# Output products laid out by rows of tokens, with norms along the free axis and h turned back by transposes

## The chip, the cores and the metric

One core of a Trainium2 chip (trn2) runs one program. The metric is the device time of that program in microseconds (us), the median of a few runs; lower is better. TensorE (PE) does the matrix products, VectorE (DVE), ScalarE (ACT) and GpSimd (POOL) the rest, and SyncE (SP) issues the weight transfers. All data are fp32.

## The reference, cut to what matters

Sequence 512, model width 1024, batch 1. Two layers of one block (three mixing branches, then a gated feed-forward net), then two layers of another (three branches only). What the change touches is what stands at the end of each of the six sub-layers, and at the start of the next:

```
for l in range(2):                          # first block
    h = rmsnorm(x, norm_mix_pre[l])
    ... three branches from h @ w_in[l] ...
    merged = g0 * y_ret + g1 * y_sc + g2 * y_cf
    x = x + rmsnorm(merged @ w_o[l], norm_mix_post[l])
    h = rmsnorm(x, norm_ffn_pre[l])
    up = causal_dwconv(h @ w_up[l], ffn_conv_w[l])        # 2 * 2816 wide
    gate, val = split(up)
    x = x + rmsnorm((silu(gate) * val) @ w_down[l], norm_ffn_post[l])
for l in range(2):                          # second block
    h = rmsnorm_2(x, pre_norm_g[l])
    ... three branches from h @ w_in[l], merged ...
    x = x + rmsnorm_2(merged @ w_out[l], post_norm_g[l])

rmsnorm(x, g) = x * rsqrt(mean(x * x over the 1024 channels) + 1e-6) * g
```

## The kernel before, in words

**Products.** Every fp32 product is made of three passes of a faster 32-bit format (F32R): each operand is split into a high and a low part, and `three` issues high x high, high x low and low x high into one PSUM bank. A weight chunk (128 x 1024 fp32, 512 KB) goes one road: SP loads it into one of 4 `raw` buffers when the low part of the chunk 4 before is cut; ACT casts the high part into one of 4 places (L903); DVE subtracts to get the low part (L1319). A place comes free when the last matmul on the chunk that was in it is done ("closed"). ACT and DVE work in program order, and cut chunks `LA` = 2 ahead of the product that they stand beside.

**Layout.** x, h and all tiles lie with the channels across the partitions: 8 tiles of 128 channels x 512 tokens. A product tile is 128 output channels x 512 tokens; weights are stationary, tokens move.

**Boundaries.** Between two sub-layers stands a boundary, numbered B = 0 to 6 in the code: 0 is the start (x to h), 1 and 3 follow the mixers of the first block, 2 and 4 its feed-forward nets, 5 and 6 the layers of the second block. At each of 1 to 6 the output product (`wo`, or `dn` for the feed-forward net) gives y; its squares are summed over the channels, which here lie across partitions. So ACT squares each tile (L1007), DVE adds them up (L1453), TensorE sums over the partitions with products by ones (`columns`, 128x1), DVE and POOL make the root on a column (L1334, L1829: a power of -0.5), and TensorE spreads it again over the partitions (`rows`, 128x128, against the identity). Then DVE renews x (L1423, L1426). The same chain with x in place of y gives h: squares on ACT (L967), sums on POOL (L1903), then h times the gain on DVE (L1437), its high part on ACT (L975), its low part on DVE and POOL (L1329, L1908).

**Order by hand.** The chain is run twice, for tokens 0 to 255 (hf = 0) and 256 to 511 (hf = 1). The first 2 output tiles (5 after a feed-forward net, `NFULL`) are made whole, the rest in halves of 256 tokens: first all left halves, then all right ones, beside which the steps of the first half's chain stand, one at each point (`beside_tail`). The weights of these tiles are kept (`KEPT`) or, after a feed-forward net, loaded twice (chunks `dn..b`). Some low parts of chunks are cut by POOL there (L1841, `POOL_LOW`). When the output product is over, three products of the next sub-layer are made early (`EARLY`): their first half (`early_first`) covers the chain of the second half, then `early_second` does the other half, k by k over all three.

After boundaries 1 and 3 follow the products `upg0`, `upv0`, `upg1`, ... of the feed-forward net. ACT's order there is: scaled copies of `upg0` and `upv0` (L1115), a sigmoid (L1120), the high part of the product of both (L980, which waits for the taps on DVE, L1583, and for POOL's L1971), and only then the casts of the next chunks. After boundaries 4 and 5 follow `cq0` to `cq2`, `ckv0`, `ckv1`: ACT copies the tiles, squares those of `cq`, POOL adds the squares (L1879), and TensorE's `columns` for them stands ahead of its product `ckv1`.

## Time and profile before

| | us |
|---|---|
| median of 3 runs | 3441.5 (3439.97 to 3445.51) |
| the profiled execution | 3445.09 |
| its span in the profile | 3443.7 |
| TensorE busy (matmuls) | 3328.8 (97%) |
| VectorE busy | 1801.6 (52%) |
| ScalarE busy | 1228.6 (36%) |
| GpSimd busy | 465.0 (14%) |

The span runs from the first to the last instruction of one execution. TensorE is busy in nearly all of it, so the time is its work plus the places where it waits. Its matmuls overlap in the records: the pace is read from the starts of neighbours, not from the length of one. PEclk is the clock that TensorE was granted, as a share of full speed (0.5 is 1.2 GHz, 1.0 is 2.4 GHz).

### The profile page before, as it was taken

How to read it: one execution, taken by the hardware profiler on the slowest of the kernel's cores; microseconds unless marked ns; L12 is line 12 of the kernel's file. 1: busy time of each engine (PE TensorE's matmuls, PEld its weight loads, DVE VectorE, ACT ScalarE, POOL GpSimd, SP SyncE). 2: the span in 40 equal slices, each digit the busy share in tenths (PEclk: the TensorE clock that was granted, in tenths of full speed). 3: DMA queues.
4: the chain of work that ended last, by engine and by line, in shares of the span. 5: the costliest groups of instructions: out<-in, count | busy, mean ns of one | idle time of the engine just before them, and what ended most of it. 6: DMA issues, size and time to landing. Idle time of an engine off the chain costs nothing.

```text
span 3443.7 us, 38725 instructions
## 1 busy us (share of the span) xinstructions
PE 3328.8 (97%) x15780; PEld 2743.6 (80%) x15780; DVE 1801.6 (52%) x2514; ACT 1228.6 (36%) x1886; POOL 465.0 (14%) x398
## 2 busy tenths in 40 slices
PE   7999989999899998999989999999998999999998
PEld 6788888888778888888877678888887658888887
DVE  3784556653577555665354442446545444344744
ACT  3232344333323234433343232226534332223742
POOL 2101121100310112111041000110013000011000
PEclk9999999999999999999999999999999999999999
DMA  4223212233322322223321132323231113222222
GB/s 147 68 80 104 92 68 92 98 104 118 112 70 78 104 95 70 92 98 100 118 93 54 53 104 86 103 81 101 89 108 60 54 62 104 88 96 87 96 93 76
DMA packets 90049, 309.81 MB, mean 90 GB/s; under 512 B 10160, under 2 KB 10416, under 8 KB 89872
## 3 DMA queue, kind: packets, MB, share of 16 engines
q1 hardware_dynamic: 87552, 299.50, 26.4%
q0 software_dynamic: 2320, 7.82, 0.7%
q8 instruction: 127, 2.08, 0.3%
q14 instruction: 50, 0.41, 0.0%
HBM read 305.18 MB, written 2.10 MB: 89 GB/s over the span
## 4 chain that ended last, share of the span: by engine, by line
PE 90%; DVE 4%; ACT 3%; POOL 2%; issue 1%; DMA 0%; SPq 0%; POOLq 0%; DVEq 0%; ACTq 0%
PE ps L454 90%; POOL f L1903 1%; ACT wh L903 1%; DVE wl L1319 1%; DVE X L1426 1%; DVE f L1423 0%; ACT r L975 0%; DVE r L1329 0%; PE ps L798 0%; DVE f L1437 0%; POOL sm L1829 0%; ACT f L1176 0%; DMA raw<-wst 0%; ACT r L980 0%; POOL wl L1841 0%
## 5 line engine op out<-in xcount | busy, mean ns | idle before, releaser
L454 PE MATMUL ps<-r,wh 128*128 128x512 f32 (+1 forms) x8584 | 2530.1, 379 | 35.6 <-DVE r L1329 22.5
L454 PEld LDWEIGHTS ps<-r,wh 128*128 128x128 f32 x8584 | 1588.1, 191 | 333.2 <-issue 34.0
L454 PE MATMUL ps<-r,wl 128*128 128x512 f32 (+1 forms) x4292 | 1617.3, 377 | 0.0
L454 PEld LDWEIGHTS ps<-r,wl 128*128 128x128 f32 x4292 | 820.4, 191 | 145.1
L1319 DVE TENSOR_TENSOR wl<-raw,wh 128x1024 fp32r<-128x1024 f32 (+3 forms) x565 | 700.4, 1255 | 326.3 <-ACT wh L903 324.9
L903 ACT CAST wh<-raw 128x1024 fp32r<-128x1024 f32 (+3 forms) x574 | 564.2, 999 | 598.6 <-PE ps L454 597.4
L980 ACT CAST r<-f 128x512 fp32r<-128x512 f32 x182 | 112.0, 620 | 508.1 <-DVE f L1590 146.8
L1500 DVE TENSOR_TENSOR f<-f,ps 128x512 f32<-128x512 f32 x96 | 66.0, 688 | 388.7 <-PE ps L454 386.3
L1941 POOL TENSOR_TENSOR f<-f,f 128x512 f32<-128x512 f32 x64 | 114.5, 1791 | 752.4 <-DVE f L1500 752.4
L1329 DVE TENSOR_TENSOR r<-f,r 128x512 fp32r<-128x512 f32 (+1 forms) x230 | 150.2, 658 | 120.9 <-ACT r L980 115.8
L454 PE MATMUL ps<-f,f 128*128 128x128 f32 (+7 forms) x640 | 201.6, 450 | 7.6 <-DVE f L1661 4.3
L454 PEld LDWEIGHTS ps<-f,f 128*128 128x128 f32 (+1 forms) x640 | 105.9, 198 | 105.9 <-issue 79.9
L1343 DVE SCALAR_TENSOR_TENSOR f<-f,vt,f 128x511 f32<-128x511 f32 (+29 forms) x240 | 174.7, 791 | 0.0
L1583 DVE SCALAR_TENSOR_TENSOR f<-ps,vt,f 128x511 f32<-128x511 f32 (+1 forms) x176 | 131.4, 748 | 73.6 <-ACT f L1115 70.5
L454 PE MATMUL ps<-wh,r 128*128 128x512 f32 x448 | 143.2, 397 | 0.0
L987 ACT COPY f<-ps 128x512 f32<-128x512 f32 x100 | 58.3, 588 | 196.7 <-PE ps L454 196.7
L1453 DVE TENSOR_TENSOR f<-f,f 128x256 f32<-128x256 f32 (+1 forms) x72 | 37.2, 516 | 162.6 <-ACT f L1007 162.3
L454 PE MATMUL ps<-r,r 128*128 128x256 f32 x960 | 118.4, 284 | 0.0
L454 PEld LDWEIGHTS ps<-r,r 128*128 128x128 f32 x960 | 116.5, 192 | 0.3
L1971 POOL TENSOR_TENSOR f<-f,f 128x512 f32<-128x512 f32 x44 | 56.6, 1287 | 411.7 <-DVE f L1583 411.7
L999 ACT ACTIVATE f<-ps,vt 128x256 f32<-128x256 f32 (+1 forms) x78 | 40.8, 523 | 192.3 <-PE ps L454 192.0
L1115 ACT ACTIVATE f<-ps,vt 128x512 f32<-128x512 f32 x88 | 60.2, 687 | 135.1 <-PE ps L454 135.1
(132 smaller groups left out, 1786.2 us busy)
## 6 DMA issues: line engine op xcount, KB each, us to landing
raw<-wst SPq DMA_DIRECT2D x500, 512.0 KB, 3.3
raw<-wst SPq DMA_DIRECT2D x48, 320.0 KB, 3.0
raw<-wst SPq DMA_DIRECT2D x38, 384.0 KB, 3.1
f<-tab POOLq DMA_DIRECT2D x16, 256.0 KB, 4.5
X<-x_in SPq DMA_DIRECT2D x4, 512.0 KB, 6.4
f<-gmb POOLq DMA_DIRECT2D x4, 512.0 KB, 4.4
raw<-wst SPq DMA_DIRECT2D x8, 256.0 KB, 3.0
out<-X SPq DMA_DIRECT2D x8, 256.0 KB, 2.0
```

The source lines that it names most:

```text
L454: return e.matmul(o, a, b, start=start, stop=stop, skip_group_check=True)
L903: e.copy(h[:, 0:WIDTH[c]], raw[:, c % NRAW, 0:WIDTH[c]]).then_inc(*hi_cut.up(("hi", c)))
L980: e.copy(r, f).then_inc(*act_hi.up(event))
L987: e.copy(dst, bank(key)).then_inc(*act_tile.up(event, ("free", key)))
L1115: e.activation(F(60 + 3 * (j % 3) + m), bank(key), ACT.Copy, scale=vec1(L, "fcw", 3 * (22 * m + j) + 2)[:, 0:1]).then_inc(*act_tile.up(("f ...
L1319: e.tensor_tensor(l[:, 0:WIDTH[c]], raw[:, c % NRAW, 0:WIDTH[c]], h[:, 0:WIDTH[c]].bitcast(F32), ALU.subtract).then_inc(*lo_cut.up(("lo", c)))
L1329: e.tensor_tensor(lo, f, hi.bitcast(F32), ALU.subtract).then_inc(*dve_lo.up(event))
L1343: e.scalar_tensor_tensor(out=C, in0=F(16 + j)[:, 0:S - s], scalar=vec1(L, "cfw", 31 * j + i)[:, 0:1], in1=C, op0=ALU.mult, op1=ALU.add).th ...
L1500: e.tensor_tensor(F(M + j) if begins else q, q, bank(key), ALU.mult).then_inc(*dve_tile.up(("free", key), *events))
L1583: e.scalar_tensor_tensor(out=q[:, s:S], in0=bank(key)[:, 0:S - s], scalar=vec1(L, "fcw", 3 * (22 * m + j) + 2 - s)[:, 0:1], in1=q[:, s:S], ...
L1941: e.tensor_tensor(F(M + j), F(M + j), F(ring[j % 3]), ALU.add).then_inc(*pool_sum.up(*events))
L1971: e.tensor_tensor(F(t + 1), F(t), F(t + 1), ALU.mult).then_inc(*pool_tile.up(("f_prod", L, j)))
```

## The change

The output products are turned round. The tokens (128 of them) are the stationary operand and 512 columns of the weights move, so y comes out as rows of tokens: 4 tiles t of 128 tokens, each in two banks n of 512 channels. x is stored so from the start (`x_in` and `out` are laid out so too). The norms are then sums along the free axis: ACT squares and sums in one instruction (`accum_out`), DVE adds the two halves and epsilon (`mean`), POOL takes the root of one column (`roots`), and DVE applies it as a scalar of each partition, with gains that are loaded as rows (`gains`, 1 MB a boundary, 0.5 MB at boundary 0). `columns` and `rows` are gone from the boundaries, and so is POOL's share of sums and low parts. h comes out as rows too, and is turned back by transposes on TensorE, 8 a tile and 32 a boundary (`turn_rows`); ACT and DVE cut its parts straight from PSUM.

The products go over tiles 0 and 1 first, then over 2 and 3. For `wo` the 8 chunks stay in place for both passes (5 in kept places, 3 in the ring). The feed-forward net's `dn` has 22 chunks of 1024 columns, one for each k, and all are read twice (44 instead of 33 chunks; of the 33, 11 had 768 columns). Four products of the next sub-layer are made early instead of three, and `early_second` goes over the products by halves of k, so that they end one after the other.

```diff
-NFULL = {1: 2, 2: 5, 3: 2, 4: 5, 5: 2, 6: 2}
-DN_PARTS = (range(0, 8), range(8, 16), range(16, 22))
+NF = 22
+WO = [(c, n) for c in range(4) for n in range(2)]
...
+    def output(L, w, l):
+        for c, n in WO:
+            out.append((f"{L}/wo{c}{n}", [(w, l, (2 * c + i) * P, P, rng(512 * n, 512)) for i in range(2)]))
...
+        for hf in range(2):
+            for k in range(NF):
+                out.append((f"{l}/dn{hf}_{k}", [("w_down", l, k * P, P, (0, 1024))]))
...
-EARLY = {0: ["0/ca0", "0/cb0", "0/ca1"], 1: ["0/upg0", "0/upv0", "0/upg1"], 2: ["1/ca0", "1/cb0", "1/ca1"],
...
-POOL_LOW = _pool_low()
+EARLY = {0: ("0/ca0", "0/cb0", "0/ca1", "0/cb1"), 1: ("0/upg0", "0/upv0", "0/upg1", "0/upv1"),
...
+         4: ("2/cq0", "2/cq1", "2/cq2", "2/ckv0"), 5: ("3/cq0", "3/cq1", "3/cq2", "3/ckv0")}
+ROWS_AT = {"y": 0, "new0": 1, "new1": 3, "x0": 5, "x1": 7, "turn0": 7, "turn1": 8, "lo0": 9, "lo1": 10}
...
             def early_second(B):
-                for k in range(8):
-                    xh, xl = h_half(B, 1, k)
+                for a in range(2):
                     for name in EARLY[B]:
                         h, l = split_at(NAME[name])
-                        last = three(bank(name)[:, halves(1)], h[:, k * P:(k + 1) * P], l[:, k * P:(k + 1) * P], xh, xl,
-                                     k == 0, k == 7)
-                        if k == 7:
+                        for k in range(4 * a, 4 * a + 4):
+                            xh, xl = h_half(B, 1, k)
+                            last = three(bank(name)[:, halves(1)], h[:, k * P:(k + 1) * P], l[:, k * P:(k + 1) * P], xh, xl,
+                                         k == 0, k == 7)
+                        if a:
                             banks.let_go(name)
                             last.then_inc(*group_done.up(("done", name), ("closed", NAME[name])))
+            def turn_rows(B, t):
+                H = ROWS_T[B][2]
+                for a in range(2):
+                    key = ("tr", B, t, a)
+                    o = take_from(key, ("y", B, t, a)) if B else take(key)
+                    w.wait_ge(*at("landed", "cst"))
+                    w.wait_ge(*at("h_out", B, t, a))
+                    for i in range(4):
+                        last = e.transpose(o[:, i * P:(i + 1) * P], F(H[a])[:, i * P:(i + 1) * P], ident)
+                    last.then_inc(*group_done.up(("done", key)))
+            def rows_by(B, t, n, ks, xs, h, l, cols, last_k, closes=None):
+                ts = slice(t * P, (t + 1) * P)
+                for k, c in zip(ks, cols):
+                    last = three(bank(("y", B, t, n)), xs[k][0][:, ts], xs[k][1][:, ts], h[:, c:c + S], l[:, c:c + S],
+                                 k == 0, k == last_k)
...
+                if B in FFN:
+                    for k in range(NF):
+                        dn(B, xs, (0, 1), k)
+                    rows((2, 3))
+                    for k in range(NF - 4):
+                        dn(B, xs, (2, 3), k)
+                        for t in range(2):
+                            if k == ROWS_AT[f"turn{t}"]:
+                                turn_rows(B, t)
+                    for t in (2, 3):
+                        for k in range(NF - 4, NF):
+                            dn(B, xs, (t,), k)
+                else:
+                    for c, n in WO:
+                        wo(B, xs, (0, 1), c, n)
+                    rows((2, 3))
+                    for c, n in WO:
+                        wo(B, xs, (2,), c, n)
+                    if B < 6:
+                        turn_rows(B, 0)
+                    for n in range(2):
+                        for c in range(4):
+                            wo(B, xs, (3,), c, n)
+                        if n == 0 and B < 6:
+                            turn_rows(B, 1)
+                if B < 6:
+                    after(B, ("e0", "e1", "e2", "t2", "t3", "e3") if B in FFN else ("e0", "t2", "e1", "e2", "t3", "e3"))
...
+            def squares(B, t, kind):
+                for n in range(2):
...
+                    e.activation(F(ROWS_T[B][3]), bank(key) if kind == "y" else xt(t, n), ACT.Square, scale=1.0 / 32,
+                                 accum_out=stat(t)[:, m:m + 1]).then_inc(*act_square.up(("squares", kind, B, t, n)))
+            def h_hi(B, t):
+                for a in range(2):
+                    w.wait_ge(*at("done", ("tr", B, t, a)))
+                    e.copy(parts(0, t, a), turned(("tr", B, t, a))).then_inc(*act_hi.up(("h_hi", B, t, a)))
...
+            def mean(B, t, kind):
+                m = 0 if kind == "y" else 4
+                w.wait_ge(*at("squares", kind, B, t, 1))
+                e.tensor_scalar(stat(t)[:, m + 2:m + 3], stat(t)[:, m:m + 1], stat(t)[:, m + 1:m + 2], EPS, ALU.add,
+                                ALU.add).then_inc(*dve_col.up(("mean", kind, B, t)))
+            def renew(B, t):
+                w.wait_ge(*at("root", "y", B, t))
+                w.wait_ge(*at("landed", f"gain{B}"))
+                for n in range(2):
...
+                    e.scalar_tensor_tensor(out=F(T[n]), in0=bank(key), scalar=stat(t)[:, 3:4], in1=gain(B, 0, n), op0=ALU.mult,
+                                           op1=ALU.mult).then_inc(*dve_tile.up(("y_out", B, t, n), ("free", key)))
+                    e.tensor_tensor(xt(t, n), xt(t, n), F(T[n]), ALU.add).then_inc(*dve_tile.up(("x_new", B, t, n)))
+            def h_out(B, t):
+                H = ROWS_T[B][2]
+                w.wait_ge(*at("root", "x", B, t))
...
+                for n in range(2):
+                    if t:
+                        w.wait_ge(*at("done", ("tr", B, t - 1, n)))
+                    e.scalar_tensor_tensor(out=F(H[n]), in0=xt(t, n), scalar=stat(t)[:, 7:8], in1=gain(B, 1, n), op0=ALU.mult,
+                                           op1=ALU.mult).then_inc(*dve_tile.up(("h_out", B, t, n)))
+            def h_lo(B, t):
+                for a in range(2):
...
+                    e.tensor_tensor(parts(1, t, a), turned(key), parts(0, t, a).bitcast(F32), ALU.subtract).then_inc(
+                        *dve_lo.up(("h_lo", B, t, a), ("free", key)))
...
+            def boundary(B):
...
+                    mean(B, 2, "y")
+                    cut(e0 + 1)
+                    renew(B, 2)
+                    cut(e0 + 3)
+                    mean(B, 3, "y")
+                    mean(B, 2, "x")
+                    renew(B, 3)
+                    h_out(B, 2)
+                    mean(B, 3, "x")
+                    h_out(B, 3)
+                    h_lo(B, 2)
+                    h_lo(B, 3)
+                    return
...
+            def roots(B, *which):
+                for kind, t in which:
+                    root(stat(t)[:, m:m + 1], stat(t)[:, m + 1:m + 2], 1, at("mean", kind, B, t), ("root", kind, B, t))
+            def gains(B):
+                e.dma_start(F(ROWS_T[B][0], 4), gains_in[B]).then_inc(*landed(f"gain{B}"))
```

On TensorE, at the end of the first feed-forward net's output product, where its last right half is followed by the second half's chain (the one product of ones, the one spread) and by `early_second`, stood:

```order
L454 MATMUL ps<-r_512_66,wh 128x256
L454 MATMUL ps<-r_512_65,wl 128x256
L454 MATMUL ps<-ct,f_512_85 128x1 x2
L454 MATMUL ps<-ct,sm 128x128 x2
L454 MATMUL ps<-r_512_51,wh 128x256
L454 MATMUL ps<-r_512_52,wh 128x256
L454 MATMUL ps<-r_512_51,wl 128x256
```

In the same place of the changed kernel the third early product is followed by the transposes of tiles 2 and 3 (L550, from the tiles of h by rows) and by the first half of the fourth:

```order
L445 MATMUL ps<-h_8192_52,wh 128x256 x2
L445 MATMUL ps<-h_8192_52,wl 128x256
L550 MATMUL ps<-ct,f_512_56 128x128 x4
L550 MATMUL ps<-ct,f_512_127 128x128 x4
L550 MATMUL ps<-ct,f_512_56 128x128 x4
L550 MATMUL ps<-ct,f_512_127 128x128 x4
L445 MATMUL ps<-h_8192_52,wh 128x256 x2
L445 MATMUL ps<-h_8192_52,wl 128x256
```

The two places where TensorE met the chain have become two sets of transposes, next to each other, ahead of the last 24 matmuls that can cover anything.

On ScalarE, in the same stretch, the last steps of both chain halves stood so (L903 casts a chunk, L999 and L1007 take a last half of y, L962 and L967 square x, L975 cuts h):

```order
L975 CAST r_512_65<-f_512_67 128x256
L999 ACTIVATE f_512_186<-ps,vt 128x256
L1007 ACTIVATE f_512_84<-ps 128x256
L903 CAST wh<-raw 128x1024
L962 ACTIVATE f_512_85<-X 128x256
L967 ACTIVATE f_512_50<-X 128x256
L967 ACTIVATE f_512_67<-X 128x256
```

and now stand so, from the last casts of `dn` on (L893 casts a chunk, L956 squares, from `ps` for y and from `X` for x, L962 cuts h):

```order
L893 CAST wh<-raw 128x1024 x9
L956 ACTIVATE f_512_71,sm<-ps 128x512 x2
L893 CAST wh<-raw 128x1024 x2
L956 ACTIVATE f_512_71,sm<-X 128x512 x2
L893 CAST wh<-raw 128x1024 x2
L956 ACTIVATE f_512_71,sm<-ps 128x512 x2
L956 ACTIVATE f_512_71,sm<-X 128x512 x2
L962 CAST h_8192_52<-ps 128x4x128 x4
```

The squares of y of tile 3 (the third L956 row) stand behind the squares of x of tile 2 and behind two casts.

## Rows read from the trace of the kernel before

**Rows 1.** Page, part 4: the chain that ended last, by engine
```profile
PE 90%; DVE 4%; ACT 3%; POOL 2%; issue 1%; DMA 0%; SPq 0%; POOLq 0%; DVEq 0%; ACTq 0%
```

**Rows 2.** Windows of boundaries 1, 2, 5, 6 and 0
```profile
core 0: us, PE busy (x) PEld busy (x) DVE busy (x) ACT busy (x) POOL busy (x), PEclk, DMA share, GB/s
440.77:522.64 81.87, 70.83 (x513) 67.53 (x512) 43.56 (x86) 35.31 (x73) 21.04 (x27) 0.96 0.19 65
748.68:910.43 161.75, 150.69 (x904) 136.21 (x902) 71.81 (x105) 56.41 (x93) 33.77 (x38) 0.96 0.35 116
...
2536.22:2620.52 84.30, 71.92 (x514) 68.38 (x512) 46.60 (x104) 36.29 (x76) 22.09 (x29) 0.94 0.23 75
3382.67:3435.15 52.48, 48.62 (x353) 45.73 (x351) 21.43 (x40) 17.69 (x35) 3.09 (x3) 0.99 0.09 30
13.18:42.58 29.40, 21.70 (x124) 20.04 (x125) 16.13 (x30) 13.58 (x29) 16.09 (x22) 0.88 0.28 92
```

**Rows 3.** Timeline of TensorE in boundary 1: start, us, engine, operation
```profile
445.54 0.40 PE L454 MATMUL ps<-r,wl 128*128 128x512 f32 x1
...
453.06 0.39 PE L454 MATMUL ps<-r,wl 128*128 128x512 f32 x1
453.28 14.55 PE L454 MATMUL ps<-r,r 128*128 128x256 f32 x120
```

**Rows 4.** Groups by line and shape, whole run: count, busy us, mean ns
```profile
L454 PE MATMUL ps<-ct,f 128*128 128x1 f32 x208 | 28.9, 256 | 35.8 <-POOL f L1903 23.1 <-DVE f L1453 9.8 <-POOL f L1879 2.9
L798 PE MATMUL ps<-ct,f 128*128 128x128 f32 x160 | 21.3, 275 | 3.2 <-DVE f L1686 3.1
L1176 ACT ACTIVATION_READ_ACCUMULATOR f<-ps,sm 128x1 f32 x64 | 13.0, 203 | 0.0
L1007 ACT ACTIVATE f<-ps 128x512 f32<-128x512 f32 x12 | 7.1, 590 | 0.0
L980 ACT CAST r<-f 128x512 fp32r<-128x512 f32 x182 | 112.0, 620 | 508.1 <-DVE f L1590 146.8 <-POOL f L2003 139.8 <-DVE f L1752 51.3
L903 ACT CAST wh<-raw 128x1024 fp32r<-128x1024 f32 x480 | 496.8, 1046 | 518.0 <-PE ps L454 516.9 <-DMA raw<-wst 1.0
L1319 DVE TENSOR_TENSOR wl<-raw,wh 128x1024 fp32r<-128x1024 f32 x474 | 613.3, 1307 | 273.3 <-ACT wh L903 272.5
L1637 DVE SCALAR_TENSOR_TENSOR f<-f,ps 128x512 f32<-128x512 f32 x16 | 11.0, 688 | 49.2 <-ACT f L1143 49.2
L1829 POOL TENSOR_TENSOR sm<-sm 128x2 f32<-128x2 f32 x24 | 18.2, 759 | 250.6 <-DVE sm L1334 250.6
L1887 POOL TENSOR_TENSOR sm<-sm 128x1 f32<-128x1 f32 x8 | 12.2, 1529 | 141.7 <-DVE sm L1401 141.7
```

**Rows 5.** Timeline of boundary 2, at the first half's root
```profile
869.78 0.89 POOL L1829 TENSOR_TENSOR sm<-sm 128x2 f32<-128x2 f32 x1
870.82 1.20 PE L454 MATMUL ps<-ct,sm 128*128 128x128 f32 x4 [2.85 <-POOL sm L1829]
871.66 0.77 PE L454 MATMUL ps<-r,wh 128*128 128x256 f32 x2
```

**Rows 6.** Timeline of the first feed-forward net's start
```profile
528.60 1.04 ACT L903 CAST wh<-raw 128x1024 fp32r<-128x1024 f32 x1
...
531.00 0.70 PE L454 MATMUL ps<-r,wh 128*128 128x512 f32 x2 [2.73 <-issue]
```

**Rows 7.** Timeline of the second block's first layer, its start
```profile
1778.19 2.87 POOL L1879 TENSOR_TENSOR f<-f,f 128x512 f32<-128x512 f32 x2 [9.02 <-ACT f L945]
...
1781.20 1.03 PE L454 MATMUL ps<-ct,f 128*128 128x1 f32 x8 [1.46 <-POOL f L1879]
```

**Rows 8.** DMA view of the first 45 us, rate in 40 slices
```profile
GB/s 0 63 330 211 291 368 284 386 334 416 422 411 379 149 269 266 233 164 0 0 0 0 0 0 0 0 222 244 0 0 0 0 0 0 15 0 66 335 244 306
```

**Rows 9.** Window inside boundary 2, where halves take whole chunks
```profile
832.00:857.00 25.00, 25.00 (x208) 24.71 (x207) 13.01 (x17) 10.72 (x17) 3.82 (x3) 1.00 0.50 166
```

**Rows 10.** Timeline of the end: the last renewal of x
```profile
3441.19 0.42 DVE L1426 TENSOR_TENSOR X<-X,f 128x256 f32<-128x256 f32 x1
```

More of the change, by code:

```diff
@@ L1020, in boundary @@
[L1020 to L1028 removed]
+                e0 = NAME[EARLY[B][0]] if B < 6 else len(CHUNKS)
@@ L1484, in gate_proj @@
+                cut(e0 + 3)
+                mean(B, 3, "y")
+                renew(B, 3)
+                mean(B, 3, "x")
+                h_lo(B, 2)
+                h_out(B, 3)
+                h_lo(B, 3)
             def gate_proj(L, b, g, p, first=0, kind="one", cut_merged=None):
```

608 lines of the change are left out of this document (238 added, 370 removed).

## The prediction

> **What bounds the kernel now.** I read the chain of waits first: TensorE is 90% of it [rows 1], so a change pays where TensorE works less or waits less, and nowhere else. The change is all at the boundaries, so the next view is the busy time in a window around each [rows 2], from the first matmul of the output product to the last of the early products. Then the pace. Between two records of the same kind lie 33 matmuls of 512 columns: (453.06 - 445.54) / 33 = 0.228 us each; 120 matmuls of 256 columns take 14.55 us, 0.121 each [rows 3]. Two halves cost 0.014 us more than a whole. At 0.228, `wo` needs 192 matmuls of 512 columns and three early products 72: 264 x 0.228 = 60.2 us. `dn` needs 528, with the early ones 600 x 0.228 = 136.7. What a window is longer than that is the price of the boundary:
>
> - 1: 81.9 - 60.2 = 21.7. 3 repeats it within 0.1 us.
> - 2: 161.8 - 136.7 = 25.1. 4 repeats it within 0.2 us.
> - 5: 84.3 - 60.2 = 24.1.
> - 6: 52.5 - 43.8 = 8.7, no early products.
>
> That is 126 us. Idle TensorE is the larger part (81.9 - 70.8 = 11.0 us in boundary 1, 11.1 in 2, 12.4 in 5, 3.9 in 6) [rows 2]. The rest is small products (28.9 us for 208 of one column, 0.14 each [rows 4]; a boundary has 16 records of them and 16 of the spreads, some 4 us), halves (2 to 3 us), and a slow clock.
>
> **The clock.** The granted clock is 0.94 to 0.96 in those windows [rows 2]; at 0.96, 8% of 82 us ran at the lower level of 1.2 GHz, which loses 3 us. It shows behind the waits: TensorE stood 2.85 us for the root until 870.82, and right behind it two matmuls of 256 columns take 0.77 us [rows 5], where the pace above is 0.24. In boundary 6, whose idle time is 3.9 us in all, the clock stayed at 0.99 [rows 2].
>
> **The change part by part.**
>
> *Removed.* All of the price above, in all boundaries: products by ones, spreads, the waits around them, the halves of the output products, the low parts on POOL.
>
> *Transposes.* 32 at each of boundaries 0 to 5. The 160 of the trace keep TensorE busy for 21.3 us, 0.133 each [rows 4]: 4.3 us a boundary. The Trainium skill ("TensorE: Matmul & The Clock Gate", Part 4: PE-mode transpose) gives some 275 ns for a transpose in a kernel's context. The trace has the mean of 275 ns for one record too, but 160 of them overlap to 21.3 us, so the record's length is not the pace; by the page's figure the 192 would cost 27 us more than in my sum.
>
> *Early products.* Four in halves: 192 matmuls of 256 columns, 192 x 0.007 = 1.3 us over whole ones. The fourth product itself is work taken from behind the boundary.
>
> *Waits in the wo boundaries (1, 3, 5).* Time 0 is the end of the pass over tiles 0 and 1; tile 2 takes 48 matmuls, 10.9 us. Squares with a sum: 0.59 + 0.20 each half [rows 4], 1.8 us a tile with the wait between; both tiles done at 3.8. `mean` on DVE is a column operation, 0.15; POOL's root 0.76 (another form with one column has 1.53, both in [rows 4]; I take 0.76, the same line's, and keep 0.8 us x 4 roots on the chain as the upper end). `renew` is four DVE operations of 0.69: tile 0 at 7.0, tile 1 at 9.8. `mean` and root of x: 11.0. `h_out` 11.7 and 12.5. TensorE wants to turn tile 0 at 10.9: it waits about 1.5 us. Tile 1 is ready when wanted. The end of the product is at about 25; on DVE the chain of tile 3 then runs squares 27.0, root 29.0, renewal 31.8, squares of x 32.8, root 34.1, low parts of tile 2 34.5, `h_out` 35.9. Covered are 4 x 2.9 us of early products less the last: TensorE is at 34.7 and waits 1 us. The first output tile, which before needed all eight merged tiles at once, now needs the last two only in its seventh chunk. With a margin of 1.5 us for hand-overs I take 4 us idle, and the clock of boundary 6, since the idle time is that of boundary 6. Price: 4.3 + 1.3 + 4 = 9.6.
>
> *Waits in the FFN boundaries (2, 4).* ACT does the squares of y of tile 3 only behind the squares of x of tile 2, and behind two casts. With time 0 at the end of the product: cast of the first early chunk at -3.5 (its place closes at -4.1), second cast done at -1.4, their low parts on DVE (1.3 us) done at +0.1, renewal of tile 2 at 2.9, its squares at 3.9, two casts of 1.05 [rows 4] at 6.0, squares of y of tile 3 at 7.8, root 9.1, renewal 12.1, `h_out` of tile 2 13.5, of tile 3 16.2. TensorE has three halves of 2.9 us: it is done at 9.3 (0.6 waited for a chunk), waits 3.7 for tile 2 and 1.4 more for tile 3, and only then comes the fourth half. Idle 6.2, with hand-overs 7, and behind a wait of 3.7 the clock falls as it does in [rows 5]: 2.5 us. Price: 4.3 + 1.3 + 7 + 2.5 = 15.1.
>
> *The chunks.* 44 in place of 33 a net. A chunk now carries 12 matmuls, 2.7 us. ACT's cast is 1.05 and DVE's 1.31 of that [rows 4]. In the window from 832 to 857 halves already took a chunk of 1024 columns in 24 x 0.121 = 2.9 us, TensorE was busy in all of it at 166 GB/s [rows 9], and the transfers of the start ran at over 400 GB/s [rows 8]. 512 KB in 2.7 us is 192 GB/s. In the second pass DVE's steps stand between the cuts; the tightest low part is done 0.8 us ahead of its use. I cost it at nothing; if that cover is gone, each 0.1 us a chunk costs 88 x 0.1 = 9 us.
>
> *Behind the boundary.* What follows is now late. The fourth early product used to cover (5.5 us) what ACT has to do before the next cast. Boundaries 1 and 3: before, the cast began at 528.60 and TensorE waited until 531.00, 2.7 us [rows 6]; that is 8.4 us from the end of the early products at 522.64 [rows 2]. Now `upv0` ends 2.9 us before the boundary's end and its taps are on DVE 1 us sooner: ready 4.7 us after it. 2 us more, and 1.5 for the clock: 3.5 each. Boundary 2: 0.3. Boundaries 4 and 5: POOL's sums of squares end at 1781.06 and TensorE had waited 1.46 us with `ckv0` before it [rows 7]. From the last copy of `cq` to there are 6 us; `cq2` now ends 1.5 us before the boundary's end, so TensorE stands 5.2 us with nothing: 3.7 more, 1.3 for the clock: 5 each.
>
> *Boundary 0.* Before, 42.6 - 13.2 us [rows 2], with three products. Now rows are normed as they land, but ACT's and DVE's orders put the first casts between the tiles; tile 3's transposes are at about 29 and the four products end at about 48, which is 42.6 plus the fourth product. Nothing.
>
> *Boundary 6.* TensorE ends 8.7 us sooner less 0.4 for a chunk: 8.3. From its last matmul the span had 8.5 us, of them a renewal in 16 small steps to 3441.6 [rows 10]. Now squares 1.8, mean, root 1.1, renewal 2.8, transfer 2.5: the same.
>
> **The sum.** 1 and 3: 21.7 - 9.6 - 3.5 = 8.6 each, 17.2. 2: 25.1 - 15.1 - 0.3 = 9.7. 4: 25.2 - 15.1 - 5 = 5.1. 5: 24.1 - 9.6 - 5 = 9.5. 6: 8.3. 0: 0. Together 49.8. The profiled execution took 3445.1 us, so 3395; it lay 3.6 us above the median of the runs, so against the median 3391.5. I say 3391.
>
> Bounds: the transposes at 0.12 (a matmul of 256 columns) to 0.14 (one of one column) -2 to +1; the squares' sum at nothing more than the copy's 0.59, -2 a boundary, the casts out of PSUM with a stride at 0.59 to 1.05, up to +2 a boundary, +10; roots at 1.53 +3 a boundary, +18; idle at nothing, -25 with its clock; the second pass short of chunks by a cover of 0.1 us, +9. Not all fall together: the forecast's own range is 3372 to 3410.
>
> **The rivals.**
>
> *The chain is not shorter, only elsewhere (half the gain).* For it: each tile crosses ACT, DVE, POOL, DVE, ACT, DVE, POOL, DVE, TensorE, ACT, DVE, and each queue holds it behind other steps; four tiles instead of two halves. Against it: tiles 0 and 1 are hidden by whole passes, and only tile 3's chain is bare. With 5 us more idle and 2 us more slow clock in five boundaries: 35 us given back, 3426.
>
> *Slower: the ring of chunks.* The feed-forward products wait for weights, one chunk after another, since a raw buffer comes free only when DVE has cut the chunk 4 before. It decides from the chunk's own time: 49.8 / 88 = 0.57, so a supply slower than 2.7 + 0.57 = 3.3 us a chunk, or 159 GB/s, eats all, and at 3.6 us a chunk the kernel takes 88 x 0.9 - 50 = 29 us more, 3471. For it: no stretch before has ever wanted 192 GB/s for 120 us. Against it: [rows 9] held 166 GB/s with TensorE full.
>
> *More than that: the waits vanish.* If the hand-overs are as short as the best of the trace, only transposes and halves stay: 3391 - 25 = 3366.
>
> *It does not do what it says.* If the order of rows did not let tile 0 and 1 go ahead (their renewal stuck in DVE's queue behind cuts that wait for places), the boundary has the chain of all four tiles bare: about 20 us idle each, no gain, 3440.
>
> **How the numbers follow.** Forecast 0.60 (3391); half the gain 0.22 (3426); waits vanish 0.09 (3366); ring 0.05 (3471); no effect 0.04 (3440). Range 3366 to 3428: it leaves out the ring, no effect, and parts of the other two. A measurement here tells 0.2%, 7 us. Faster needs less than 3434.6: the forecast, the waits gone and nearly all of the half gain, 0.91. Same: most of the no-effect case, 0.04. Slower 0.05.
>
> **What would show it.** Windows of the same shape around the boundaries: longer than 60.2 by about 10 us for `wo`, than 136.7 by 15 for `dn` (one more early product adds 5.5 to each). TensorE waits ahead of L550: 1.5 us once in a wo boundary, near 4 and 1.4 in an FFN one, with ACT's L956 on `ps` in front of them. A wait of nearly 5 us at each start of `ffn` and 5 us ahead of the `cq` sums. No wait of a `wh,r` product for L893 or L1305 inside `dn`. The forecast is wrong in its largest term if such waits appear in `dn`, or if the waits ahead of L550 sum to over 10 us.

## The result, and the profile after

| | before | after |
|---|---|---|
| median, same chips | 3443.09 us (4 runs) | 3366.84 us (4 runs, 3362.54 to 3367.42) |
| the profiled execution, its span | 3445.09, 3443.7 | 3367.42, 3366.1 |
| mean granted clock of TensorE | 0.982 | 0.989 |

The ratio is 0.9776, with a 95% interval of 0.9759 to 0.9793: 76 us faster, where 50 were forecast. Against the 3441.5 us that the prediction was worked out from, that ratio gives 3364.4. The busy times and the chain of waits of the changed kernel (L445 is `three`, L893 the cast, L1305 the low part, L1424 `h_out`, L550 the transposes):

```profile
PE 3296.2 (98%) x14952; PEld 2681.3 (80%) x14952; DVE 1795.5 (53%) x2353; ACT 1212.4 (36%) x1800; POOL 363.3 (11%) x288
...
PE 94%; DVE 2%; ACT 2%; issue 1%; POOL 0%; DMA 0%; SPq 0%; ACTq 0%; POOLq 0%; DVEq 0%
```

TensorE's share of the chain went from 90% [rows 1] to 94%, and DVE, ACT and POOL together from 9% to 4%. TensorE's busy time fell too (3328.8 to 3296.2 us). Windows of boundaries 1, 2, 5, 6 and 0, cut as in [rows 2] from the first matmul of the output product to the last early one:

```profile
435.83:506.43 70.60, 70.53 (x417) 62.33 (x415) 39.47 (x57) 28.51 (x55) 8.89 (x11) 1.00 0.27 90
731.69:885.67 153.98, 148.72 (x753) 126.95 (x751) 82.75 (x92) 66.93 (x92) 10.01 (x17) 0.99 0.54 179
2483.23:2553.83 70.60, 70.52 (x417) 62.32 (x415) 39.61 (x71) 29.89 (x58) 9.64 (x12) 1.00 0.31 104
3314.90:3358.78 43.88, 43.80 (x193) 35.77 (x191) 17.92 (x24) 11.34 (x21) 3.88 (x5) 1.00 0.26 96
12.30:48.59 36.29, 32.23 (x224) 30.65 (x225) 16.61 (x24) 14.72 (x25) 5.11 (x10) 1.00 0.41 150
```

These hold four early products: 288 x 0.228 = 65.6 us are needed in a `wo` window, 624 x 0.228 = 142.3 in a `dn` window. The price of a boundary is now 70.6 - 65.6 = 5.0 us in 1, 3 and 5 (forecast 9.6) and 154.0 - 142.3 = 11.7 in 2, 11.5 in 4 (forecast 15.1). In a `wo` window TensorE is busy in all but 0.1 us, at the full clock.

Stage by stage, from the start of each output product to the next (the last to the end of the span):

| from, to | before | after | change | forecast |
|---|---|---|---|---|
| start, B1 | 440.8 | 435.8 | -4.9 | 0 |
| B1, B2 | 307.9 | 295.9 | -12.1 | -8.6 |
| B2, B3 | 555.6 | 541.4 | -14.2 | -9.7 |
| B3, B4 | 307.9 | 295.4 | -12.5 | -8.6 |
| B4, B5 | 924.0 | 914.7 | -9.3 | -5.1 |
| B5, B6 | 846.5 | 831.7 | -14.8 | -9.5 |
| B6, end | 61.0 | 51.2 | -9.8 | -8.3 |

Together -77.6 us of span against -49.8 forecast. Each stage gave more than forecast, by 1.5 to 5.3 us.

The transposes in boundary 1, on TensorE:

```profile
468.37 0.62 PE L445 MATMUL ps<-r,r 128*128 128x512 f32 x2
468.83 1.03 PE L550 MATMUL ps<-ct,f 128*128 128x128 f32 x8
469.62 0.48 PE L445 MATMUL ps<-wh,r 128*128 128x512 f32 x1
```

No idle time stands before them. From the first of 8 to the next product are 0.79 us, 0.099 each; one follows the other at 0.109, and `double_turn` below gives 0.11 for one more. I count 0.11. In boundary 2 (TensorE, then ACT, then POOL) two waits are left:

```profile
864.08 0.28 PE L445 MATMUL ps<-h,wl 128*128 128x256 f32 x1
866.70 1.23 PE L550 MATMUL ps<-ct,f 128*128 128x128 f32 x8 [2.34 <-DVE f L1424]
868.81 1.97 PE L550 MATMUL ps<-ct,f 128*128 128x128 f32 x8 [0.89 <-DVE f L1424]
870.43 0.78 PE L445 MATMUL ps<-h,wh 128*128 128x256 f32 x2
871.00 0.41 PE L445 MATMUL ps<-h,wl 128*128 128x256 f32 x1
```

```profile
858.18 0.63 ACT L956 ACTIVATE f<-X 128x512 f32<-128x512 f32 x1 [0.66 <-DVE X L1415]
...
858.81 1.98 ACT L893 CAST wh<-raw 128x1024 fp32r<-128x1024 f32 x2
860.70 0.58 ACT L956 ACTIVATE f<-ps 128x512 f32<-128x512 f32 x1
...
861.40 0.60 ACT L956 ACTIVATE f<-ps 128x512 f32<-128x512 f32 x1
```

```profile
867.41 0.55 POOL L1851 TENSOR_TENSOR sm<-sm 128x1 f32<-128x1 f32 x1 [3.91 <-DVE sm L1402]
```

The order on ACT is the one that the prediction named: squares of x of tile 2, two casts, then the squares of y of tile 3. The matmuls behind the wait show the clock: two of 256 columns in 0.57 us, start to start, where [rows 3] have 0.24. Behind boundary 1 stands what [rows 6] had, and there is a wait near the start of `dn` that the prediction did not have (TensorE, and ACT at the second place):

```profile
506.31 0.28 PE L445 MATMUL ps<-h,wl 128*128 128x256 f32 x1
511.17 1.19 PE L445 MATMUL ps<-h,wh 128*128 128x512 f32 x2 [4.59 <-issue]
512.16 0.63 PE L445 MATMUL ps<-h,wl 128*128 128x512 f32 x1
...
736.90 0.39 PE L445 MATMUL ps<-wh,r 128*128 128x512 f32 x1
739.33 0.47 PE L445 MATMUL ps<-wh,r 128*128 128x512 f32 x1 [2.04 <-ACT wh L893]
...
1727.58 0.56 PE L445 MATMUL ps<-ct,f 128*128 128x1 f32 x2 [5.21 <-POOL f L1883]
```

```profile
732.47 0.62 ACT L1104 ACTIVATE f<-f 128x512 f32<-128x512 f32 x1
736.40 0.62 ACT L967 CAST r<-f 128x512 fp32r<-128x512 f32 x1 [3.31 <-DVE f L1604]
736.93 3.88 ACT L893 CAST wh<-raw 128x1024 fp32r<-128x1024 f32 x4
```

ACT begins its sigmoid at 732.47 and then stands 3.31 us, for DVE's product of the taps, at the cast of that product (L967). Four chunk casts are queued behind it, in order, and the third chunk of `dn` is one of them. The waits behind boundaries 4 and 5 are those of [rows 7] grown from 1.46 to 5.21 us.

**Where 77.6 us came from.** TensorE idle, the span less its busy time: 3443.7 - 3328.8 = 114.9 us before, 3366.1 - 3296.2 = 69.9 after, -45. The mean clock of 0.982 before comes from 122 us at half speed, of which half is lost, 61; after there are 77 us of it, 39 lost: -22. The 192 records of small products are gone (0.111 each by `small_back` below): -21. The 192 transposes: +21. Some 970 pairs of halves in the output products are gone (0.0114 each by `halved_rows`): -11. The fourth early product is in halves: +2. That is -76. The first two terms are read from the traces, no run takes them away one by one, and they overlap a little, since a slow stretch can fall on idle time.

### The profile page after: what moved, and what is told of

Its sections match the earlier page's. It is cut to its first block, busy times and chain, and to the rows that moved or that the text cites. A ratio compares the mean times of both kernels' runs of the same rounds, so it can differ in the third digit from the quotient of the medians.

```text
span 3366.1 us, 36633 instructions
## 1 busy us (share of the span) xinstructions
PE 3296.2 (98%) x14952; PEld 2681.3 (80%) x14952; DVE 1795.5 (53%) x2353; ACT 1212.4 (36%) x1800; POOL 363.3 (11%) x288
## 4 chain that ended last, share of the span: by engine, by line
PE 94%; DVE 2%; ACT 2%; issue 1%; POOL 0%; DMA 0%; SPq 0%; ACTq 0%; POOLq 0%; DVEq 0%
PE ps L445 93%; DVE wl L1305 1%; ACT wh L893 1%; PE ps L550 1%; PE ps L792 0%; DMA raw<-wst 0%; DVE f L1597 0%; ACT f L1160 0%; DVE f L1412 0%; POOL f L1883 0%; DVE f L1359 0%; POOL f L1961 0%; ACT r L967 0%; DVE f L1424 0%; DVE f L1700 0%
## 5 line engine op out<-in xcount | busy, mean ns | idle before, releaser
L445 PE MATMUL ps<-h,wh 128*128 128x512 f32 (+1 forms) x5824 | 1717.1, 379 | 14.0 <-issue 13.0
L445 PEld LDWEIGHTS ps<-h,wh 128*128 128x128 f32 x5824 | 1074.5, 190 | 216.6 <-issue 20.4
L445 PE MATMUL ps<-h,wl 128*128 128x512 f32 (+1 forms) x2912 | 1098.4, 377 | 0.0
L1305 DVE TENSOR_TENSOR wl<-raw,wh 128x1024 fp32r<-128x1024 f32 (+3 forms) x596 | 745.3, 1265 | 358.3 <-ACT wh L893 356.7
L893 ACT CAST wh<-raw 128x1024 fp32r<-128x1024 f32 (+3 forms) x596 | 593.1, 1008 | 686.9 <-PE ps L445 671.8
L445 PEld LDWEIGHTS ps<-h,wl 128*128 128x128 f32 x2912 | 552.8, 190 | 100.1
L445 PE MATMUL ps<-r,wh 128*128 128x512 f32 x1632 | 507.3, 392 | 1.2 <-DVE f L1359 1.2
L445 PEld LDWEIGHTS ps<-r,wh 128*128 128x128 f32 x1632 | 305.3, 188 | 68.5 <-issue 6.4
L445 PE MATMUL ps<-r,wl 128*128 128x512 f32 x816 | 317.7, 389 | 0.0
L445 PE MATMUL ps<-wh,r 128*128 128x512 f32 x960 | 305.1, 392 | 4.4 <-ACT wh L893 4.1
L967 ACT CAST r<-f 128x512 fp32r<-128x512 f32 x182 | 112.1, 620 | 515.1 <-DVE f L1604 146.8
L445 PEld LDWEIGHTS ps<-wh,r 128*128 128x128 f32 x960 | 180.2, 188 | 44.7 <-ACT wh L893 4.9
L445 PE MATMUL ps<-f,f 128*128 128x128 f32 (+7 forms) x640 | 201.1, 449 | 7.6 <-DVE f L1675 4.3
L445 PEld LDWEIGHTS ps<-f,f 128*128 128x128 f32 (+1 forms) x640 | 105.8, 197 | 105.4 <-issue 79.5
L445 PE MATMUL ps<-wl,r 128*128 128x512 f32 x480 | 186.8, 389 | 0.0
L445 PEld LDWEIGHTS ps<-r,wl 128*128 128x128 f32 x816 | 153.2, 188 | 32.2
```

The source lines that it names most:

```text
L445: return e.matmul(o, a, b, start=start, stop=stop, skip_group_check=True)
L893: e.copy(h[:, 0:WIDTH[c]], raw[:, c % NRAW, 0:WIDTH[c]]).then_inc(*hi_cut.up(("hi", c)))
L967: e.copy(r, f).then_inc(*act_hi.up(event))
L1305: e.tensor_tensor(l[:, 0:WIDTH[c]], raw[:, c % NRAW, 0:WIDTH[c]], h[:, 0:WIDTH[c]].bitcast(F32), ALU.subtract).then_inc(*lo_cut.up(("lo", c)))
```

## The experiments

All times are medians beside runs of the kernel before on the same chip; ratios are against it. The changed kernel's is 0.9776. A slow stretch is time in which TensorE was granted half its clock.

**late_squares**: in boundaries, the squares of y of tiles 0 and 1 begin only when the whole pass is done.

```diff
                     if kind == "y":
+                        if t < 2:
+                            w.wait_ge(*at("done", ("y", B, 1, 1)))
                         w.wait_ge(*at("done", key))
```

> The changed kernel, in which ACT squares y of tiles 0 and 1 only when the last bank of tile 1 is done. In the changed kernel the first halves of both tiles are squared one chunk earlier, which I had left out. If an early start of the chain was all that kept TensorE from waiting ahead of the first transposes of the wo boundaries, the wait of 1.5 us that I forecast is back in boundaries 1, 3 and 5, with some slow clock: about 3372. If my durations for the chain were too long as well (roots of 0.55 us in place of 0.76, squares of 0.78 a half in place of 0.9), about 2 us of slack are left, the wait is under 0.5 us and the time stays at 3366 to 3368.

3365.9 us, ratio 0.9768 (0.9751 to 0.9784): nothing. Its chain of boundary 1, on ACT, DVE and TensorE:

```profile
458.15 0.60 ACT L958 ACTIVATE f<-ps 128x512 f32<-128x512 f32 x1 [7.81 <-PE ps L445]
...
467.58 1.41 DVE L1426 SCALAR_TENSOR_TENSOR f<-X,sm,f 128x512 f32<-128x512 f32 x2 [0.66 <-POOL sm L1853]
...
468.84 1.03 PE L550 MATMUL ps<-ct,f 128*128 128x128 f32 x8
```

From the end of the pass (435.8 + 96 x 0.228 = 457.7) `h_out` of tile 0 now ends at 469.0, 11.3 us later; the prediction had 12.5 for both halves, and a wait of 1.5. The steps were shorter than the prediction's, and the early start of the squares only adds reserve: the second of the two outcomes named.

**double_turn**: each transpose twice.

```diff
-                    for i in range(4):
+                    for i in list(range(4)) * 2:
```

> The changed kernel with each transpose of h issued twice (the second writes the same place): 192 more. If a transpose costs TensorE what its neighbours' starts show in the changed kernel (8 of them in 0.79 us, 0.10 each), 19 us more, a little less where they fall into a wait: 3383 to 3387. If it costs its record's length, 0.275 us, 53 us more: 3420.

3376.4 us, 0.9805 (0.9791 to 0.9820): 10 us more, under the 3383 to 3387 expected. In boundary 1:

```profile
468.31 1.91 PE L550 MATMUL ps<-ct,f 128*128 128x128 f32 x16
469.98 0.48 PE L445 MATMUL ps<-wh,r 128*128 128x512 f32 x1
```

16 transposes take 1.67 us where 8 took 0.79, 0.11 for each more. The span grew by 13.4 us, TensorE's idle time fell from 69.9 to 66.9, and the slow stretches from 77.3 to 75.3 us, worth 1.0: together some 17 us for 192 transposes, 0.09 each. At the record's length of 0.27 it would have been 52.

**small_back**: one fp32 product by one column and one of 128 columns put ahead of each four transposes.

```diff
+                    e.matmul(o[:, 0:1], F(H[a])[:, 0:P], ident[:, 0:1], start=True, stop=True)
+                    e.matmul(o[:, 0:P], F(H[a])[:, 0:P], ident, start=True, stop=True)
                     for i in range(4):
```

> The changed kernel with the small products put back: ahead of each set of four transposes one fp32 product by a single column and one of 128 columns against the identity, 8 of each a boundary (boundaries 0 to 5), 192 records in all, as many as the change took out of the boundaries. Their results are overwritten by the transposes. Theory (they cost TensorE only their own time, 0.10 to 0.13 us a record as the transposes do): 19 to 25 us more, less 1 to 2 us where they stand in a wait: 3384 to 3391 us. Rival (a small fp32 product between matmuls of the split format costs its record of 0.25 to 0.275 us, or the change of format costs more): 192 x 0.26 = 50 us more, 3417 us.

3380.53 us, 0.9815 (0.9802 to 0.9829): 13 us more, under the 19 to 25 expected. In boundary 1:

```profile
470.25 0.28 PE L549 MATMUL ps<-ct,f 128*128 128x1 f32 x2
...
470.69 0.60 PE L552 MATMUL ps<-ct,f 128*128 128x128 f32 x4
...
471.93 0.48 PE L445 MATMUL ps<-wh,r 128*128 128x512 f32 x1
```

Eight transposes with their eight small records take 1.68 us from the first to the next product, where the transposes alone took 0.79: 0.111 a record, as the theory has it. The span grew by 12.4 us, idle time fell by 5.2 (69.9 to 64.7), and the slow stretches fell from 77.3 to 74.5 us, worth 1.4: 19 us together for 192 records, 0.10 each. So the size per record holds; what the forecast had too small was the idle time that the small products would fill (1 to 2 us). The clock moves the time on its own, too: matmul by matmul the run is 17.3 us behind the changed kernel at 2713 us and 12.4 at 2770, because the changed kernel has a slow stretch of 10.2 us there that this one has not.

**halved_rows**: each output-product matmul as two of 256 columns. Its output products are not the sums of the reference; number and shape of its matmuls are as the edit says.

```diff
+                    for q in (0, 256):
-                    last = three(bank(("y", B, t, n)), xs[k][0][:, ts], xs[k][1][:, ts], h[:, c:c + S], l[:, c:c + S],
+                        last = three(bank(("y", B, t, n))[:, q:q + 256], ..., h[:, c + q:c + q + 256], l[:, c + q:c + q + 256],
...
```

> The changed kernel with every output-product matmul of 512 columns made as two of 256 columns (1824 of them become 3648). This sizes the term of halves that the change took out of the output products. Theory (pace 0.228 us for 512 columns, 0.121 for 256, so 0.014 us a pair): 1824 x 0.014 = 25.5 us more, about 3392 us, and the windows of the output products longer by 2.7 us (wo, 192 pairs) and 7.4 us (dn, 528 pairs). Rival (a half costs more than the pace of 256 columns shows, because each needs its own weight load of 128 columns, which no longer hides): 0.03 us a pair or more, over 3421 us.

3388.63 us, 0.9835 (0.9822 to 0.9849): 20 us more. Its boundary 6:

```profile
3327.65:3373.72 46.07, 46.07 (x385) 46.02 (x383) 17.92 (x24) 11.32 (x21) 3.88 (x5) 1.00 0.24 92
```

46.07 - 43.88 = 2.2 us for 192 pairs, 0.0114 a pair (0.014 forecast), and 1824 x 0.0114 = 21 us. The halves' own weight loads stay hidden (46.02 us of them within 46.07 of matmuls).

**three_early**: three early products, in the old order of `early_second`, all else as changed.

```diff
-EARLY = {0: ("0/ca0", "0/cb0", "0/ca1", "0/cb1"), 1: ("0/upg0", "0/upv0", "0/upg1", "0/upv1"),
+EARLY = {0: ("0/ca0", "0/cb0", "0/ca1"), 1: ("0/upg0", "0/upv0", "0/upg1"),
...
-                    after(B, ("e0", "e1", "e2", "t2", "t3", "e3") if B in FFN else ("e0", "t2", "e1", "e2", "t3", "e3"))
+                    after(B, ("e0", "e1", "e2", "t2", "t3") if B in FFN else ("e0", "t2", "e1", "e2", "t3"))
...
```

> The changed kernel with three early products and the old order of early_second (k by k over all three). If the row layout makes the gain, and the fourth product mostly moves waits: each of boundaries 1 to 5 waits about 2.5 us for the cuts of tile 3's h, but the starts behind the boundaries wait 2.9 and 1.6 us instead of 4.6 and 5.3 and keep the faster clock: within 10 us of the changed kernel either way, 3356 to 3376. If the fourth product is what pays, 15 to 30 us of the gain are lost: 3382 to 3397.

3353.28 us, 0.9736 (0.9722 to 0.9751): 14 us faster than the changed kernel, and 3 us under the 3356 to 3376 of the first outcome. At the end of boundary 1 and behind it:

```profile
492.94 0.47 PE L445 MATMUL ps<-h,wh 128*128 128x256 f32 x2 [0.95 <-DVE h L1431]
...
503.53 0.70 PE L445 MATMUL ps<-h,wh 128*128 128x512 f32 x2 [1.72 <-DVE f L1597]
...
510.02 0.70 PE L445 MATMUL ps<-h,wh 128*128 128x512 f32 x2 [0.78 <-issue]
```

Three short waits in place of one of 4.59, and after none of them the matmuls run at half pace (0.70 us for two here, 1.19 there). The mean clock is 0.992 against 0.989. So the fourth early product, as it was built in and with the order of `early_second` that came with it, cost 14 us. The two were not taken apart.

**before_four**: the kernel before with four early products and their `early_second`; the fourth product's chunk is cut just ahead of the step that makes h of the second half.

```diff
-EARLY = {0: ["0/ca0", "0/cb0", "0/ca1"], 1: ["0/upg0", "0/upv0", "0/upg1"], 2: ["1/ca0", "1/cb0", "1/ca1"],
+EARLY = {0: ["0/ca0", "0/cb0", "0/ca1", "0/cb1"], 1: ["0/upg0", "0/upv0", "0/upg1", "0/upv1"],
...
+                early_first(B, 3)
+                for step in steps[xrow:]:
```

> The kernel before with that part alone: four early products, early_second by halves of k, one product after the other; the fourth stands ahead of the spread of the root of x. If the fourth product is what pays: 3443 - 20 = 3423. If the row layout pays and this moves waits: a microsecond or two less in each boundary, 2 to 5 us more behind boundaries 1, 3, 4 and 5: 3438 to 3452.

3475.68 us, 1.0092 (1.0077 to 1.0107): 32 us slower, far outside what was expected. Around boundary 1 the waits up to the last products by ones are all still there, with one of 0.5 us more. The 1.13 us before the last spread is gone, but 1.43 us stands in its place, ahead of the fourth product, and the 1.56 us behind the spread is still there (TensorE, and DVE's low part of the fourth product's chunk):

```profile
514.80 0.47 PE L455 MATMUL ps<-r,wh 128*128 128x256 f32 x2 [1.43 <-issue]
521.43 0.48 PE L455 MATMUL ps<-r,wh 128*128 128x256 f32 x2 [1.56 <-DVE r L1336]
```

```profile
513.49 1.21 DVE L1326 TENSOR_TENSOR wl<-raw,wh 128x1024 fp32r<-128x1024 f32 x1
```

The profile names no releaser for the 1.43, but the low part ends at 514.70 and TensorE begins at 514.80, and in boundaries 2 to 5 it is the same to 0.1 us: most likely the fourth product came too late for its own chunk, by this edit's order. Behind boundaries 1 and 3 stand 4.58 us and behind 4 and 5 5.20, as in the changed kernel. Idle time grew by 15 us (114.9 to 129.9) and slow stretches by 19 (122 to 141), worth 9.5. These and the halves of the fourth product are 26 of the 30 us of its span; the rest was not placed. So the run shows that this fourth product does not pay in the kernel before, not that none could.

**ffn_cut**: ACT and DVE cut one more chunk ahead of the wait for the taps (both engines, one line each).

```diff
                             *act_tile.up(("f_tap", L, j, m, 0)))
+                    cut(NAME[f"{L}/upv{j}"] + LA + 1)
                     w.wait_ge(*at("f_tap", L, j, 0, 2))
...
```

> The changed kernel; in each step j of the feed-forward net ACT and DVE cut the next chunk right after the copy and the taps of upv_j, and no longer behind the product's high and low part. Theory: the wait of 4.6 us behind boundaries 1 and 3 is ACT's queue order (the cast stands behind a wait for DVE and POOL), and so is the wait of 2.2 us at the third chunk of dn. Then both go down to under 1 us, with the slow clock behind the first: 12 us of waits and 3 to 6 of clock, 3348 to 3353. Rival: the chunk's place or its transfer comes late: no change, 3366.

3347.04 us, 0.9722 (0.9708 to 0.9737): 0.0054 of 3443, or 19 us faster, a little more than expected. TensorE behind boundary 1, and ACT in front of it:

```profile
505.58 0.70 PE L445 MATMUL ps<-h,wh 128*128 128x512 f32 x2 [0.66 <-issue]
```

```profile
502.68 1.04 ACT L893 CAST wh<-raw 128x1024 fp32r<-128x1024 f32 x1
503.61 0.64 ACT L1105 ACTIVATE f<-f 128x512 f32<-128x512 f32 x1
507.45 0.62 ACT L967 CAST r<-f 128x512 fp32r<-128x512 f32 x1 [3.20 <-DVE f L1606]
```

ACT waits as long as before, but the cast stands ahead. TensorE's 4.59 became 0.66, and the 2.04 in `dn` is gone as well: one cause for both, twice each. The four waits together shrank by 11.9 us, and the slow stretches from 77 to 60 us, worth 9.

**norm_shift**: the sums for the `cq` norm taken a few products later.

```diff
-                tile(f"{L}/ckv1", xs)
-                tile(f"{L}/kr", xs)
+                tile(f"{L}/ckv1", xs, beside=False)
+                small_step("n_root", L, "q")
+                tile(f"{L}/kr", xs, beside=False)
+                small_step("n_apply", L, "q")
```

> The changed kernel; in the second block TensorE's steps of the q and k norms (products by ones, spreads) stand one product later each. Theory: the wait of 5.3 us behind boundaries 4 and 5 is for POOL's sums, while ckv1 could run; its own chunk is there 1 to 2 us after the boundary. Then the wait is 1 to 2 us, and with less slow clock 3353 to 3359. Rival: ckv1 has to wait for its chunk as long, or the wait moves to the next product: 3363 to 3367.

3354.92 us, 0.9743 (0.9729 to 0.9758): 11 us faster. Of the 5.21 us, twice, what is left there, on TensorE:

```profile
1723.03 0.70 PE L445 MATMUL ps<-h,wh 128*128 128x512 f32 x2 [1.49 <-ACT wh L898]
```

**ffn_order**: in boundaries 2 and 4, squares of y of tile 3 ahead of those of x of tile 2, one cast between, with VectorE's cuts moved to match; tile 3 is turned behind the fourth half.

```diff
-                    after(B, ("e0", "e1", "e2", "t2", "t3", "e3") if B in FFN else ("e0", "t2", "e1", "e2", "t3", "e3"))
+                    after(B, ("e0", "e1", "e2", "t2", "e3", "t3") if B in FFN else ("e0", "t2", "e1", "e2", "t3", "e3"))
...
                     cut(e0 + 1)
+                    squares(B, 3, "y")
+                    cut(e0 + 2)
                     squares(B, 2, "x")
...
```

> The changed kernel with another order at the end of dn: ACT squares y of tile 3 before x of tile 2, each chunk is cut in a step of its own, and TensorE makes the fourth early product between the transposes of tiles 2 and 3. Theory: the waits of 2.4 and 1.05 us there are queue order on ACT and DVE, not the length of the chain: together under 1.5 us, and one slow clock period less in each: 3358 to 3363. Rival: the chain of tile 3 is too long for its cover in any order: the wait moves to early_second, 3365 to 3368.

3358.39 us, 0.9757 (0.9741 to 0.9774): the 2.34 and 0.89 of boundary 2 became one of 1.05 behind the last transposes:

```profile
866.48 1.04 PE L550 MATMUL ps<-ct,f 128*128 128x128 f32 x8
868.57 0.48 PE L445 MATMUL ps<-h,wh 128*128 128x256 f32 x2 [1.05 <-DVE h L1432]
```

By the ratios it is 7 us, but its interval and that of the changed kernel overlap, so the waits show the effect better than the time does.

**all_three**: the last three edits together.

> The three edits together (chunks cut ahead in the feed-forward net, the norms' steps one product later, the order at the end of dn). If the three waits are independent, the sum: about 3334 (3328 to 3342). If they hide one another (a slow clock period counted twice, one queue's order upset by the next edit), above 3345.

3331.39 us, 0.9676 (0.9661 to 0.9690), mean clock 0.994. By the ratios the three gains alone add up to 0.0106, or 36 us; together they give 0.0100, 34 us. This is the fastest version, 3.2% under the kernel before:

```profile
PE 3283.3 (99%) x14952; PEld 2669.3 (80%) x14952; DVE 1792.2 (54%) x2353; ACT 1209.7 (36%) x1800; POOL 407.2 (12%) x288
```

**three_tuned**: three_early with the edits of ffn_cut, and ACT's and DVE's order of ffn_order. (In its text the comparison is with all three edits; norm_shift's is not in this run.)

> Three early products instead of four, with the order of ScalarE and VectorE of the two edits that helped four (the second cut of a feed-forward step ahead of its wait, and tile 3's squares of y ahead of tile 2's squares of x in the feed-forward boundaries). It asks whether a fourth early product is worth its place once the waits behind it are mended: with four and all edits the median was 3331.4 us. Theory (the fourth product covers the chain of tile 3, and only its side effects made it lose): three products keep waits of 1 to 2.4 us before the transposes, so 3340 to 3347 us, slower than with four. Rival (three are enough in themselves; the clock and the chain profit from the shorter list): 3332 us or less.

3340.51 us, 0.9698 (0.9684 to 0.9711), as the first theory has it. It keeps waits of 1.35 and 1.23 us around the transposes of both feed-forward boundaries, and 1.72 behind boundaries 1 and 3. Four early products with all edits are 0.0022 of the ratio, 7.6 us, better; the two intervals overlap from 0.9684 to 0.9690. Some of this may be norm_shift's, whose place had a wait of 1.18 us here. Most likely the fourth product is worth a few us once the order around it is mended; where it is not, it costs 14.

## Why the prediction was right or wrong

**Right.** The sign, and where the time was: each boundary, and not the chunks. `dn` ran at 179 GB/s over its whole window with TensorE busy in 148.7 of 154.0 us, so, but for the cast of its third chunk (below), the supply of chunks never held it, and the profile puts no wait of TensorE down to a transfer. The wait behind boundaries 1 and 3 was forecast at 4.7 and came at 4.6, that behind 4 and 5 at 5.2 and came at 5.2: both were worked out by following what the last early product's copy must do on ACT and POOL. (The terms given for the first, 8.4 - 2.9 - 1, make 4.5.) The order on ACT that makes the waits of boundary 2 was named. The Trainium skill ("TensorE: Matmul & The Clock Gate", Part 4) gives 275 ns for a transpose in a kernel's context, there of bf16. That is the length of one fp32 record here (0.27 us), so the page and the trace agree on the record; the prediction was right not to price by it, since one more transpose costs TensorE 0.11 us.

**Wrong in size: 50 us forecast, 76 measured.** 3366.84 us is the bottom edge of the stated range of 3366 to 3428, and the 3364.4 of the ratio lies below it. The mechanism held and terms of the sum were mis-sized. The step that failed most is the idle time with its margin in the `wo` boundaries: 4 us each, measured 0.1. By windows, the 27.8 us of span that the sum missed are 3 x (9.6 - 5.0) = 13.8 in the `wo` boundaries, 3.4 + 3.6 = 7.0 in the feed-forward ones, 4.9 up to boundary 1, and 1.5 from boundary 6 on; what is left, 0.6, lies behind the boundaries. Nearly all were priced from above:

- *Idle time in the `wo` boundaries, 4 us each: 1.5 for tile 0, 1 for tile 3, 1.5 of margin.* It was 0.1. The chain's clock failed. For tile 0, from the end of the pass: squares done at 3.8 (late_squares: 3.3), roots 0.76 each (0.55), `h_out` 12.5 (11.3). For tile 3, `h_out` was done at 33.8 against 35.9. The prediction took a root's price from two columns, though the kernel's own has one, and then added a margin for hand-overs to durations that already held them. 12 us over three boundaries.
- *Transposes at 0.133.* 0.11: 0.7 us a boundary, 3.7 in the five that the sum prices. The busy time of 160 records holds the tail of each group's last record (0.27 us long) besides the pace. The bound of 0.12 was wrong too; in the kernel before the 160 already followed each other at 0.109.
- *Idle time in the FFN boundaries, 7 us and 2.5 for the clock.* 2.34 + 0.89, and the clock at half for 3.4 us, which loses 1.7: the same chain steps, done early (`h_out` of tile 2 at 11.7 us from the product's end against 13.5, of tile 3 at 13.9 against 16.2), and the 0.6 us wait for a chunk did not occur.
- *Boundary 0, costed at nothing.* -3.8 us at its end, -4.9 up to the first `wo`. The kernel after was forecast well (48, measured 48.6), the one before was misread. The window in [rows 2] was cut at 42.58, but the last spread stands inside the second early product, whose third goes on to 46.90:

```profile
32.70 1.05 PE L454 MATMUL ps<-ct,sm 128*128 128x128 f32 x4
33.41 0.77 PE L454 MATMUL ps<-r,wh 128*128 128x256 f32 x2
...
46.78 0.28 PE L454 MATMUL ps<-r,wl 128*128 128x256 f32 x1
46.90 0.63 PE L454 MATMUL ps<-r,wh 128*128 128x512 f32 x2
```

  46.9 + 24 x 0.228 = 52.4, against 48.6 now. The end of a window has to be found by its matmuls' shape (x256 turns to x512), not by a count from the last spread.
- *The wait of 2.04 at the third `dn` chunk* (twice) was missed, in the other direction; the prediction had named such a wait inside `dn` as a sign against itself. It looked for trouble inside the second pass; it lies where two steps of ACT's queue meet, and a chunk there now lasts TensorE 12 x 0.228 = 2.7 us, where one of the first whole tiles lasted 24 x 0.228 = 5.5 and so covered it (that the length of the chunk makes the difference is argued, no run tests it). That the wait and the one behind boundary 1 have one cause is shown by ffn_cut.
- *The clock behind waits.* Forecast as costs of 1.5 and 1.3 us; behind boundary 1 it was 3.4 (half speed for 6.8 us). But the clock elsewhere gave back more: slow stretches fell from 122 us to 77 over the run. The prediction priced the clock only in the boundaries and right behind them.
- *Boundary 6, 8.3.* 9.8: its window came out 0.3 us better, and from TensorE's last matmul to the end are 7.3 us where there were 8.5, which the prediction had as the same.

The rival "the waits vanish" named the time to within 1 us (3366), and that was luck: its reason holds only for `wo`. 70 us of idle time are left in the whole run, 23 of which the three edits remove, and boundaries 0 and 6, which it does not touch, gave 6 us. The rival "half the gain" is out by 60 us. The fourth early product, which the prediction valued at nothing in the sum and as cover for tile 3, was the part of the change that cost: 14 us by three_early.

## What to carry to other kernels

Before you cost a chain of small steps, read each step's duration in its own shape and its start-to-start distance; do not add a margin on top. When work is moved ahead to cover one wait, list what was hidden behind it: here the in-order queue of ACT held a ready cast behind a step that waited 3.0 and 3.3 us, and one line more on each of two engines was worth 19 us. And a long wait costs more than itself where the clock falls behind it: 4.59 us was followed by matmuls at half pace, while waits of 0.95, 1.72 and 0.78 us, some 10 us apart, were not.
